# Delta rule: decay rows read back from DRAM instead of broadcast products, and keys multiplied by the state before the inverse

## The reference, cut to what matters

```python
G = jnp.cumsum(g, axis=-1)
dmat = jnp.exp(jnp.where(incl, G[..., :, None] - G[..., None, :], -jnp.inf))
kb = k * beta[..., None]
a = jnp.where(strict, jnp.einsum('bhnid,bhnjd->bhnij', kb, k) * dmat, 0.0)
t = _unit_lower_inverse(a)
u = t @ (v * beta[..., None])
w = t @ (kb * jnp.exp(G)[..., None])
kd = k * jnp.exp(G[..., -1:] - G)[..., None]
...
def step(s, inp):
    w_c, u_c, kd_c, gl_c = inp[:4]
    v_new = u_c - jnp.einsum('bhck,bhkv->bhcv', w_c, s)
    s_next = s * gl_c[..., None, None] + jnp.einsum('bhck,bhcv->bhkv', kd_c, v_new)
    ...
    o_c = jnp.einsum('bhck,bhkv->bhcv', qg_c, s) + jnp.einsum('bhij,bhjv->bhiv', qa_c, v_new)
```

## Time and profile before

| | us |
|---|---|
| median of 3 runs | 2399.29 |
| span of the profiled execution | 2402.4 |
| of it: stage dn_delta, first matmul to last output product | 250.9 to about 524 |
| PE busy over the span | 2261.8 |
| DVE busy over the span | 1400.0 |
| ACT busy over the span | 919.3 |

### The profile page before, as it was taken

One profiled execution on the slowest core, in us unless ns is written; L12 is line 12 of the kernel. 1 busy time (PEld: TensorE's weight loads), 2 busy tenths in 40 slices (PEclk: granted clock), 3 DMA queues, 4 the chain that ended last, 5 costly groups with the idle time before them and its releaser, 6 DMA issues. The chain is left out here.

```text
span 2402.4 us, 44900 instructions
## 1 busy us (share of the span) xinstructions
PE 2261.8 (94%) x17672; PEld 1746.9 (73%) x17672; DVE 1400.0 (58%) x2663; ACT 919.3 (38%) x1712; POOL 110.8 (5%) x142
## 2 busy tenths in 40 slices
PE   6999899999889999999999998999999989999996
PEld 3885799986546888888888886875665558666663
DVE  3694666654899777777777776765321166552123
ACT  4463344331159555555555554453110135321111
POOL 1000000000000000000000000100111010011110
PEclk8998999999979999999999999999999999999999
DMA  8236200026778655555555566612999984159997
GB/s 312 85 140 211 108 3 3 2 105 238 241 254 296 200 189 189 189 188 191 192 192 192 192 189 229 229 74 83 410 418 418 420 310 156 66 217 418 419 419 299
DMA packets 127893, 521.65 MB, mean 217 GB/s; under 512 B 18904, under 2 KB 21128, under 8 KB 98295
## 3 DMA queue, kind: packets, MB, share of 16 engines
q1 hardware_dynamic: 111902, 489.86, 54.8%
q0 software_dynamic: 15840, 29.61, 3.6%
HBM read 522.09 MB, written 26.28 MB: 228 GB/s over the span
## 5 line engine op out<-in xcount | busy, mean ns | idle before, releaser
L254 PE MATMUL PS<-over,over 128*128 128x512 f32 (+1 forms) x1056 | 387.0, 367 | 6.8 <-ACT ring L720 3.0
L256 PE MATMUL PS<-over,over 128*128 128x512 f32 (+1 forms) x1056 | 383.9, 364 | 0.0
L255 PE MATMUL PS<-over,over 128*128 128x512 f32 (+1 forms) x1056 | 383.4, 363 | 0.0
L2051 DVE TENSOR_TENSOR over<-ring,over 128x1024 fp32r<-128x1024 f32 x256 | 307.2, 1221 | 3.6 <-ACT over L2047 3.4
L3328 PE MATMUL PS<-ring 128*32 128x256 f32 (+2 forms) x2288 | 295.1, 385 | 8.1 <-DMA ring<-in_w_gate 7.9
L2047 ACT CAST over<-ring 128x1024 fp32r<-128x1024 f32 x256 | 267.9, 1047 | 66.0 <-PE PS L256 64.2
L3328 PEld LDWEIGHTS PS<-ring 128*32 128x32 f32 (+2 forms) x2288 | 212.9, 145 | 90.2 <-issue 32.5
L254 PEld LDWEIGHTS PS<-over,over 128*128 128x128 f32 x1056 | 201.6, 191 | 37.6 <-issue 6.5
L2112 PE MATMUL PS<-over,over 128*128 128x512 f32 x896 | 224.1, 389 | 2.6 <-POOLq L3467 2.6
L255 PEld LDWEIGHTS PS<-over,over 128*128 128x128 f32 x1056 | 201.0, 190 | 31.9 <-issue 0.5
L256 PEld LDWEIGHTS PS<-over,over 128*128 128x128 f32 x1056 | 200.7, 190 | 32.3
(11 more groups left out here) (532 smaller groups left out, 3184.5 us busy)
## 6 DMA issues: line engine op xcount, KB each, us to landing
ring<-in_mod_w SPq DMA_DIRECT2D x64, 1024.0 KB, 5.5
ring<-in_peer_u SPq DMA_DIRECT2D x128, 512.0 KB, 3.5
ring<-in_peer_v SPq DMA_DIRECT2D x128, 512.0 KB, 4.5
ring<-in_w_gate SPq DMA_DIRECT2D x64, 1024.0 KB, 16.7
ring<-in_w_up SPq DMA_DIRECT2D x64, 1024.0 KB, 19.2
ring<-in_w_down SPq DMA_DIRECT2D x64, 1024.0 KB, 19.6
ring<-in_w_in SPq DMA_DIRECT2D x12, 2048.0 KB, 9.2
ring<-in_dn_w SPq DMA_DIRECT2D x8, 2048.0 KB, 7.7
```

Of the source, the lines that this page charges most:

```text
L254: nc.tensor.matmul(out, lhs[0], rhs[0], start=start, stop=False)
L255: nc.tensor.matmul(out, lhs[0], rhs[1], start=False, stop=False)
L256: return nc.tensor.matmul(out, lhs[1], rhs[0], start=False, stop=stop)
L2051: nc.vector.tensor_tensor(PSPL[s % 4][0][:, 1, :], PRAW[s % 4], PSPL[s % 4][1][:, 0, :], ALU.subtract).then_inc(s_lo, 1)
```

## The change

The running sums are transposed once, in dn_unit (one transposition, a DVE copy), written to a DRAM tensor `gc_home` of 64 rows by POOL, and read back by SP for each group and direction: four rows of 128, broadcast to all partitions, 256 KB, into one buffer per direction. "sub" and "eG" read this buffer instead of PSUM. The buffer of d is loaded again when "sub" (and "eG", with queries) of the group before are done.

"Gr", "wT" and "kb" are gone. "kS" is new: keys times state, in the groups with a state; it stands where "Gr" stood, between the squares and the product of round 0, but of group gi itself. ACT scales it by -beta exp(G) per head. "vb" moves from ACT to DVE: values times beta plus kS, four operations per direction (one wide one without a state), behind product 1. "vn" is one product per head. ACT's "eG" moves behind the copy of "p" of round 1.

```diff
+        gc_rows = idx.rearrange("p a t -> p (a t)")[0:NQ * 16, 4 * P:5 * P]
+        gc_home = nc.dram_tensor("gc_home", (NQ * 16, P), F32).ap()
+        s_gc_home, s_decay = sem("gc_home"), [sem(f"decay{d}") for d in range(2)]
+        decay_rows = [arena(9216 + d * CW, 4, P) for d in range(2)]
 
...
+            dn2_dv.wait(e, "GT")
+            e.dma_start(gc_home, gc_rows).then_inc(s_gc_home, 16)
...
+            dn2_pe.wait(e, "GT")
+            dn2_dv.mark(D_.tensor_copy(gc_rows, tr_bank("GT")[0:NQ * 16, 0:P]), "GT")
             out(K[6])
...
+            bank_free("GT")
+            dn2_dv.wait(e, "Gc")
+            dn2_pe.mark(nc.tensor.transpose(tr_bank("GT")[0:NQ * 16, 0:P], Gc.rearrange("p t c -> p (t c)"), ident), "GT")
...
             take = carve(*spans)
-            B = {n: take(P) for n in ("DT", "Araw", "kb", "vb", "kd", "qg0", "qg1", "qa0", "qa1", "tf", "wT", "vn")}
+            B = {n: take(P) for n in ("DT", "Araw", "vb", "kd", "qg0", "qg1", "qa0", "qa1", "tf", "kS", "vn")}
...
+        def has_state(gi):
+            return groups[gi][0] > 0
...
-            def gram(gi):
+            def state_keys(gi):
+                for d in range(2):
+                    dl_dv[d].wait(e, (gi, "Ao"))
+                    dl_dv[d].wait(e, (gi - 2, "s"))
+                    tk = slice(tile(d, gi) * P, tile(d, gi) * P + P)
+                    for h in range(HG):
+                        ins = mm(wide(d, "kS")[:, h, :], kT[:, heads(gi), tk][:, h, :], state[:, d, heads(gi), :][:, h, :])
+                    dl_pe[d].mark(ins, (gi, "kS"))
+
+            def keys(gi):
                 for d in range(2):
                     if gi:
+                        if has_state(gi - 1):
+                            dl_ac[d].wait(e, (gi - 1, "kS"))
                         dl_dv[d].wait(e, (gi - 1, "Ao"))
-                    for h in range(HG):
-                        g = g16[:, tile(d, gi), cols(d, gi)][:, h:h + 1]
-                        ins = mm(wide(d, "Gr")[:, h, :], g.broadcast_to([P, P]), MASK["inc_" + "fb"[d]])
-                    dl_pe[d].mark(ins, (gi, "Gr"))
-
-            def keys(gi):
-                for d in range(2):
-                    dl_dv[d].wait(e, (gi, "sub"))
-                    if with_x(gi):
-                        dl_ac[d].wait(e, (gi, "eG"))
                     tk = slice(tile(d, gi) * P, tile(d, gi) * P + P)
                     for h in range(HG):
...
             def recurrence(gi):
                 for d in range(2):
+                    dl_dv[d].wait(e, (gi, "vb"))
                     dl_dv[d].wait(e, (gi, "R"))
                     for h in range(HG):
-                        ins = mm(wide(d, "wT")[:, h, :], buf[d]["kb"][:, h, :], buf[d]["tf"][:, h, :])
-                    dl_pe[d].mark(ins, (gi, "wT"))
-                for d in range(2):
-                    dl_ac[d].wait(e, (gi, "wT"))
-                    for h in range(HG):
-                        mm(wide(d, "vn")[:, h, :], buf[d]["tf"][:, h, :], buf[d]["vb"][:, h, :], stop=False)
-                        ins = mm(wide(d, "vn")[:, h, :], buf[d]["wT"][:, h, :], state[:, d, heads(gi), :][:, h, :], start=False)
+                        ins = mm(wide(d, "vn")[:, h, :], buf[d]["tf"][:, h, :], buf[d]["vb"][:, h, :])
                     dl_pe[d].mark(ins, (gi, "vn"))
...
                 n = gi + 1
                 for r in range(ROUNDS):
                     squares(gi, r)
+                    if r == 0 and has_state(gi):
+                        state_keys(gi)
                     if n < NGROUP:
-                        if r == 0:
-                            gram(n)
-                        elif r == 1:
+                        if r == 1:
                             keys(n)
...
             def decay(gi):
-                if with_x(gi):
-                    for d in range(2):
-                        dl_dv[d].wait(e, (gi, "sub"))
-                        dl_ac[d].mark(A.activation(buf[d][f"qg{gi % 2}"], wide(d, "Gr"), ACT.Exp), (gi, "eG"))
                 for d in range(2):
                     dl_dv[d].wait(e, (gi, "E"))
                     dl_ac[d].mark(A.activation(buf[d]["DT"], buf[d]["DT"], ACT.Exp), (gi, "DT"))
+
+            def q_decay(gi):
+                for d in range(2):
+                    e.wait_ge(s_decay[d], 16 * (gi + 1))
+                    dl_ac[d].mark(A.activation(buf[d][f"qg{gi % 2}"], decay_rows[d], ACT.Exp), (gi, "eG"))
+
+            def state_keys(gi):
+                for d in range(2):
+                    dl_pe[d].wait(e, (gi, "kS"))
+                    for h in range(HG):
+                        ins = A.activation(buf[d]["kS"][:, h, :], wide(d, "kS")[:, h, :], ACT.Identity,
+                                           scale=nbeG[:, tile(d, gi), cols(d, gi)][:, h:h + 1])
+                    dl_ac[d].mark(ins, (gi, "kS"))
 
...
                 n = gi + 1
                 square(gi, 0)
+                if has_state(gi):
+                    state_keys(gi)
                 if n < NGROUP:
                     decay(n)
                 square(gi, 1)
-                scaled(gi, "vb", Vrow, beta)
+                if n < NGROUP and with_x(n):
+                    q_decay(n)
                 square(gi, 2)
...
                     A.activation(sm[:, 144:145], eps_col, ACT.Sqrt)
-                evacuate(gi, "wT", None)
                 evacuate(gi, "vn", None)
 
...
             def decay(gi):
                 for d in range(2):
-                    dl_pe[d].wait(e, (gi, "Gr"))
-                    dl_dv[d].mark(V.tensor_tensor(buf[d]["DT"], wide(d, "Gr"), per_head(Gc, d, gi), ALU.subtract), (gi, "sub"))
+                    e.wait_ge(s_decay[d], 16 * (gi + 1))
+                    dl_dv[d].mark(V.tensor_tensor(buf[d]["DT"], decay_rows[d], per_head(Gc, d, gi), ALU.subtract), (gi, "sub"))
                 for d in range(2):
...
                             ins = V.tensor_tensor(buf[d]["tf"][half(u), :, half(u)], t[half(u)], packed(d, "t")[half(u)], ALU.add)
                     dl_dv[d].mark(ins, (gi, ("t", r)))
 
-            def k_scaled(gi):
+            def v_scaled(gi):
                 for d in range(2):
-                    dl_dv[d].mark(V.tensor_tensor(buf[d]["kb"], Krow[:, tile(d, gi), heads(gi), :], per_head(nbeG, d, gi), ALU.mult),
-                                  (gi, "kb"))
+                    v, b = Vrow[:, tile(d, gi), heads(gi), :], beta[:, tile(d, gi), cols(d, gi)]
+                    if has_state(gi):
+                        dl_ac[d].wait(e, (gi, "kS"))
+                        for h in range(HG):
+                            ins = V.scalar_tensor_tensor(buf[d]["vb"][:, h, :], v[:, h, :], b[:, h:h + 1], buf[d]["kS"][:, h, :],
+                                                         ALU.mult, ALU.add)
+                    else:
+                        ins = V.tensor_tensor(buf[d]["vb"], v, per_head(beta, d, gi), ALU.mult)
+                    dl_dv[d].mark(ins, (gi, "vb"))
 
             def inverse(gi):
...
                 product(gi, 0)
-                k_scaled(gi)
                 square(gi, 1)
                 if more:
                     keys(n)
                 product(gi, 1)
+                v_scaled(gi)
                 square(gi, 2)
...
+        def load_decay(sp):
+            dn2_dv.wait(sp, ("unit", 11))
+            sp.wait_ge(s_gc_home, 16)
+            for gi in range(NGROUP):
+                for d in range(2):
+                    if gi:
+                        dl_dv[d].wait(sp, (gi - 1, "sub"))
+                        if with_x(gi - 1):
+                            dl_ac[d].wait(sp, (gi - 1, "eG"))
+                    first = tile(d, gi) * 16 + cols(d, gi).start
+                    sp.dma_start(decay_rows[d].rearrange("p h t -> p (h t)"),
+                                 gc_home[first:first + HG].rearrange("h t -> (h t)").unsqueeze(0).broadcast_to([P, HG * P])
+                                 ).then_inc(s_decay[d], 16)
+        stream.append(load_decay)```

The lists of names for the semaphores follow the same order.

How the change stands in the instruction streams. In the rows of both programs L1139 (now L1157) is the full-width matmul and L1143 (L1161) the blocks of squares and products. The first place is PE, from group 4's last products to the rounds of group 5, and then the opening of the stage.

Before, from group 4's last products:

```order
L1139 MATMUL PS<-ring 128x128 x48
L1143 MATMUL PS<-ring 64x64 x32
L1139 MATMUL PS<-ring 128x128 x8
L1143 MATMUL PS<-ring 64x64 x48
L1139 MATMUL PS<-ring 128x128 x8
L1143 MATMUL PS<-ring 64x64 x48
L1139 MATMUL PS<-ring 128x128 x8
L1143 MATMUL PS<-ring 64x64 x48
```

29 lines of the change are left out of this document (16 added, 13 removed).

## The result

The changed kernel takes **2377.95 us** (median of 4 runs, 2375.74 to 2380.78), the kernel before 2400.4 (4 runs beside it, 2398.77 to 2402.5): a ratio of **0.9901, 95% interval 0.9885 to 0.9918**. That is 1% faster, by 22 us, inside the range of 2362 to 2381. Of the 32 us that the forecast (2367.2) promised, 11 are missing. The two profiled executions have spans of 2402.4 and 2379.0 us, 23.4 us apart.

A forecast was written before the change was run, and what follows sets the result against it. PE's own instruction stream was taken as the bound. 31.8 - 1.4 - 0.3 + 2.5 - 0.5 = 32.1 us off the median of 2399.29 gave 2367.2 us; stated range 2362 to 2381, the forecast's own 2363 to 2372.

The forecast's parts named there:

- the end: Stage end: the last group saves 3.7 us, but DVE's norm sums last; 3.2 gained, so 0.5 lost.
- DVE's cover: Rounds: "vb" on DVE ahead of the "q2" copies; covered in groups 3 to 6, 1.4 us lost in the others.
- ACT's scalings of "kS": Groups with a state: ACT scales "kS" from PSUM in 2.45 us, covered, so costing 0.
- The first rows: Decay rows before the stage: write 4.1 us, load 3.9, landing at 248.0 and 248.5, hidden by 2.3 us.
- The opening: Stage start: "sub" needs no PE, so the first flip comes near 254.4, 3.0 earlier; 2.5 us gained.
- PE, removed: PE's stream in the stage: "Gr" 13.9 us, "wT" 14.9 and half of "vn" 14.9 go; net 31.8 with "kS" added.
- DVE's wait: Group 0: PE reaches the squares before DVE's "q2" copy is done; 0.3 us lost.
- The clock: Rival, behind the corners: one 1.7 us dip in each other group costs 12 us, giving 2379; chance 0.09 in all.
- DVE becomes the bound: Rival, in the rounds: the 2.2 us of "vb" exposed in all six groups, giving 2379; chance 0.12.
- The first rows arrive late: Rival, before the first "sub": rows caught among the blank writes land near 261, 10 us later, giving 2377; chance 0.07.
- The loss through the clock: Rival, over the stage: half of it at 1.2 GHz gives 2487; chance 0.04 for a loss over all.
- they move as a whole: Later stages: they start from weights SP asks for when this stage ends, so they all shift together.

The follow-up runs named there:

- rows_only: The changed kernel with only the decay rows from DRAM: "kb", "wT" and the two-product "vn" kept, no "kS"; 2387.3 us.
- late_blank: The changed kernel with POOL's blank writes and the modulation read behind them put off until group 2's state is written; 2374.2 us.
- before_late: The kernel before the change with the blank writes and the modulation read put off to group 2's state; 2404.4 us.
- vb_twice: The changed kernel with DVE's scaling of the values done twice in the six groups with a state; 2388.9 us.

## Why the prediction was right, and what was off

**Direction and mechanism: right.** PE's instruction stream set the time, and each removed round was worth its start-to-start distance. Where nothing disturbed it a period gave 3.6 of 3.7 us, and with the transfers moved and no dip the whole stage gave 32.3 us for 32.4. Term by term: "Gr" 2.0 to 2.1 (rows_only) for 1.98; the product of the values and "kS" together as forecast; the flip at 254.22 for 254.4; the end 3.28 for 3.2.

**What was luck.** The forecast's own range, from the ends of its terms, was 2363 to 2372, and the median of 2377.95 is 6 us outside it. It lies inside the stated range only because that was stretched for three rivals, none of which came about as told.

**Smaller terms.** DVE's cover was forecast to fail by 1.4 us; it failed by 0.5 (0.25 in groups 2 and 7, nothing in 0 and 1). ACT's scalings of "kS" were covered, as forecast. The first rows landed earlier than costed (the write took 1.8 us for 4.1, the loads 3.1 and 3.9 for 3.9), so the margin was over 5 us, not 2.3. Those of group 1 were as near a miss as told: twice the quiet time was forecast, 2.3 and 2.8 times came.

**The step that failed** is the sum's silence on group 0: "The opening" and "PE, removed" gave the first stretch 4.5 us, 4.2 with DVE's wait; it gave 1.3, and late_blank against before_late shows that it is 4.45 once the large transfers are away. The forecast had asked what those transfers do to the decay rows, and not what they do to PE's own instructions, which come by DMA too. Its statement that a removed matmul is worth its distance holds only while the next instructions are there. Cost: 3.0 us here, 4.1 in the second profile.

**The clock** was named as a rival and priced well for a short dip (1.7 us; 1.5 and 3.1 measured, by length), but read wrongly: not the change makes the dips, and not one corner in eight has one, but about one in four, in either kernel (4 of 16 in the two profiles without the change, 5 of 16 in the two of the changed kernel). The kernel before had one in its profile, the changed one two, its repeat three. That is worth 1.5 to 9 us in these three, in which the kernels do not differ; it should have stood in the range as scatter and not as a cause.

**The rivals.** "DVE becomes the bound" gave 2379 and came near by number only; vb_twice shows a margin of 1.4 us left in groups 3 to 6. "The first rows arrive late" did not happen, and where it is made to happen it costs 13 to 14 us, not 10. The loss through the clock did not come.

**What stays open.** The rest of the program was 3.3 us longer in the profile of the changed kernel. Over the profiles of twelve variants it ran from 1870.6 to 1879.4, and from 1867.7 to 1871.3 in the two with nothing of the change in them. Only rows_only lies below those 1871.3, and the means are 1875.1 and 1869.5. So some us are probably given back behind the stage, against the forecast's "they move as a whole"; no run shows where. Open too is what sets which instruction packet is late.

## What to carry to other kernels

When matmuls are taken out of a stream that is PE-bound, ask what feeds the stream: the instructions that are left arrive by DMA, and large transfers beside them (here from 247 to 272 us) can eat a tenth of the gain. Here it helped to put them beside the instructions that last longest. Make the stage's margins (here 5 us for the rows) from measured landings. And set a stage's periods side by side before the totals: seven periods told in one look which of the terms held, while the medians scatter by more than what was sought.
